# Forgetting attention of a two-block kernel: probabilities scaled before the product with the values, or the product scaled after it

## The reference, cut to what matters

```python
for i in range(S // Q_BLOCK):                      # four query tiles of 128
    logits = einsum("bqhd,bkhd->bhqk", qb, kb) * scale
    logits = logits + cum[:, :, q0:kl, None] - cum[:, :, None, :kl]
    p = jax.nn.softmax(jnp.where(mask, logits, NEG_INF), axis=-1)
    outs.append(einsum("bhqk,bkhd->bqhd", p.astype(vb.dtype), vb))
...
u = jax.nn.silu(layer_norm(causal_depthwise_conv(a * sigmoid(g)), ...))
return jnp.concatenate([u, att], axis=-1) @ w_out
```

## Time and profile before

| what | value |
|---|---|
| median of 3 runs | 1826.43 us (1825.73 to 1826.66) |
| the profiled execution | 1825.45 us |
| its span, first to last instruction | 1823.7 us |
| TensorE busy in the span | 1778.4 us (98%) |
| VectorE, ScalarE, GpSimd busy | 57%, 25%, 59% |
| mean granted TensorE clock | 0.992 |
| the attention loop on TensorE | 122.1 us to 211.9 us |
| TensorE busy in it | 79.32 of 89.80 us |

### The profile page before, as it was taken

The page is one execution under the profiler, slowest core; times in us unless marked ns, Lnnn a source line. Parts: engine busy times, 40 slices in busy tenths (PEclk is TensorE's granted clock), DMA queues, the critical chain, the costliest instruction groups (busy, mean ns, idle before and its releaser), DMA issues.

```text
span 1823.7 us, 22550 instructions
## 1 busy us (share of the span) xinstructions
PE 1778.4 (98%) x8332; PEld 1442.7 (79%) x8332; DVE 1030.7 (57%) x1194; ACT 463.7 (25%) x931; POOL 1074.9 (59%) x604
## 2 busy tenths in 40 slices
PE   9998999999999999999999999999999999999997
PEld 7775777788888877767888888887888888888886
DVE  5989465845252675175625261696766562616177
ACT  6427334401010122163201020212336320202011
POOL 7593453566666665434666666675344566666672
PEclk9999999999999999999999999999999999999999
DMA  6231221233333332212332333332122233332331
GB/s 239 70 103 48 81 78 39 81 102 94 93 102 93 94 102 92 82 47 59 92 104 92 96 100 92 98 99 81 52 66 69 79 95 93 100 97 92 103 93 47
DMA packets 46591, 161.44 MB, mean 89 GB/s; under 512 B 5232, under 2 KB 7792, under 8 KB 46384
## 3 DMA queue, kind: packets, MB, share of 16 engines
q1 hardware_dynamic: 45088, 157.31, 28.3%
q10 hardware_dynamic: 1424, 3.02, 0.5%
HBM read 158.21 MB, written 2.10 MB: 88 GB/s over the span
## 4 chain that ended last, share of the span: by engine, by line
PE 92%; DVE 4%; ACT 2%; issue 1%; DMA 0%; POOL 0%; SPq 0%; DVEq 0%; ACTq 0%
PE bank L405 21%; PE bank L407 21%; PE bank L406 21%; PE bank L453 3%; PE bank L455 3%; PE bank L454 3%; PE bank L1031 1%; PE bank L1001 1%; PE bank L473 1%; PE bank L474 1%; PE bank L475 1%; PE bank L1003 1%; PE bank L1002 1%; DVE bank L1768 1%; PE bank L1046 1%
## 5 line engine op out<-in xcount | busy, mean ns | idle before, releaser
L319 POOL TENSOR_TENSOR WL<-RAW,WH 128x1024 fp32r<-128x1024 f32 x291 | 740.1, 2543 | 24.3
L314 POOL TENSOR_SCALAR WH<-RAW 128x1024 fp32r<-128x1024 f32 x291 | 313.9, 1079 | 680.2 <-PE bank L407 362.7
L405 PE MATMUL bank<-AH,WH 128*128 128x512 f32 x848 | 332.6, 392 | 0.0
L406 PE MATMUL bank<-AL,WH 128*128 128x512 f32 x848 | 330.0, 389 | 0.0
L407 PE MATMUL bank<-AH,WL 128*128 128x512 f32 x848 | 330.0, 389 | 0.0
L405 PE MATMUL bank<-HH,WH 128*128 128x512 f32 x832 | 325.0, 391 | 0.0
L406 PE MATMUL bank<-HL,WH 128*128 128x512 f32 x832 | 323.8, 389 | 0.0
L407 PE MATMUL bank<-HH,WL 128*128 128x512 f32 x832 | 323.7, 389 | 0.0
L1421 ACT ACTIVATE TMP<-bank 128x512 f32<-128x512 f32 x96 | 57.3, 596 | 776.7 <-PE bank L407 738.9
L2043 DVE TENSOR_TENSOR HL<-TMP,HH 128x512 fp32r<-128x512 f32 x96 | 238.9, 2488 | 3.9 <-ACT HH L1426 0.7
L2049 DVE TENSOR_TENSOR Y<-Y,bank 128x512 f32<-128x512 f32 x72 | 49.5, 687 | 309.0 <-PE bank L407 309.0
(11 more groups left out here) (388 smaller groups left out, 2371.9 us busy)
## 6 DMA issues: line engine op xcount, KB each, us to landing
RAW<-wstream SPq DMA_DIRECT2D x291, 512.0 KB, 3.6
out<-Y SPq DMA_DIRECT2D x8, 256.0 KB, 2.3
X<-xT SPq DMA_DIRECT2D x3, 512.0 KB, 8.5
TMP<-memT ACTq DMA_DIRECT2D x1, 1024.0 KB, 7.5
MIX<-bands ACTq DMA_DIRECT2D x1, 768.0 KB, 4.6
RAW<-wstream SPq DMA_DIRECT2D x2, 256.0 KB, 3.8
X<-xT SPq DMA_DIRECT2D x2, 256.0 KB, 4.2
BF<-masks ACTq DMA_DIRECT2D x1, 352.0 KB, 3.7
```

Of the source, the lines that this page charges most:

```text
L314: nc.gpsimd.tensor_scalar(WH[:, s, :, :].rearrange("p k n -> p (k n)"), RAW[:, s, :], 1.0, 1.0, ALU.mult, ALU.mult).then_inc(sem("w_high"), 1)
L319: nc.gpsimd.tensor_tensor(WL[:, s, :, :].rearrange("p k n -> p (k n)"), RAW[:, s, :], f32(WH[:, s, :, :].rearrange("p k n -> p (k n)")), A ...
L405: mm(bank, WH[:, slot, k, :], h(k), start=(k == 0), stop=False)
L406: mm(bank, WH[:, slot, k, :], l(k), start=False, stop=False)
```

## The change

The exponentials are transposed and multiplied by the values as they are. VectorE takes the reciprocals of a whole pair's eight row sums in one instruction (iterations 4, 8, 12, 16). TensorE makes rows of them: eight small matmuls for a pair (`fox_factors`, iterations 5, 9, 13, 17), whose stationary operand is a column of SUMI repeated 64 times and whose moving operand is the identity, so that bank FOX_R holds in each head's 64 partitions the factor of every query. ScalarE copies that bank to TMP (`fox_fcopy`, iterations 6, 10, 14, 18), VectorE multiplies FOX_O by it into FOX_R (`fox_normed`, iterations 7, 11, 15, 19), ScalarE takes the high part from there (`fox_out`, same iterations) and VectorE the low part one iteration later (`fox_split`). The next pair's products now wait for `fox_normed`.

Since FOX_R is bank 6 for three pairs, the gate has bank 7 alone: ScalarE's last exponential of tile c waits until u of tile c-1 is split. The twelve matmul triples of the output projection come in another order, those into bank 6 last and behind a wait for the third pair. Four more convolution taps run ahead of the loop (FRONT_TAPS 32 in place of 28). In ScalarE's iterations the convolution's tail now comes ahead of the pair's output.

```diff
--- before.py
+++ after.py
@@ -63,7 +63,9 @@
 MLPS = ["m3", "f0", "f1"]
...
 FOX_S, FOX_T, FOX_O = (4, 5, 2), 0, 1
-FRONT_TAPS = 28
+FOX_R = (6, 6, 6, 2)
+OUT_PIECES = (((0, 0), (0, 1), (0, 2)), ((0, 3), (2, 0), (2, 1)), ((2, 2), (2, 3), (1, 0)), ((1, 1), (1, 2), (1, 3)))
+FRONT_TAPS = 32
 K_BANKS = (3, 4, 1, 2)
...
 OUT_FILL = 15
@@ -93,7 +95,6 @@
 SIDE_SECOND = 6
...
 POOL_QUADS = 7
-ACT_SCALED = 6
 FAMILIES = {
...
     "ah": each(["m1", "mm", "m2", "m3", "b", "f0", "c", "f1"], "ah", 8),
@@ -118,7 +119,7 @@
...
     "exp": [(f"{p}_exp", n) for p, n in ATTS],
-    "probs": [("fox_probs", 2 * (16 - ACT_SCALED)), ("mem_probs", 16), ("dif_probs", 16)],
+    "probs": [("mem_probs", 16), ("dif_probs", 16)],
     "trans": [("fox_trans", 32), ("mem_trans", 16), ("dif_trans", 16)],
...
     "pv": [("fox_pv", 16), ("mem_pv", 16), ("dif_pv", 16)],
@@ -212,7 +213,7 @@
         VC = sb("VC", [P, NVEC])
...
         MAXI = sb("MAXI", [P, 8])
-        SUMI = sb("SUMI", [P, 8])
+        SUMI = sb("SUMI", [P, 16])
         RC = sb("RC", [P, 4])
...
@@ -626,11 +627,12 @@
                 n = U0["out"]
...
                 pe.wait_ge(sem("u_low"), nth("u_low", 4))
-                for k in range(4):
-                    if k % 2 == 0:
-                        pe.wait_ge(sem(f"raw_split{k // 2}"), nth(f"raw_split{k // 2}", n // 4 + 1))
-                    pe.wait_ge(sem("u_low"), nth("u_low", k + 1))
-                    for j in range(3):
+                pe.wait_ge(sem("raw_split0"), nth("raw_split0", n // 4 + 1))
+                pe.wait_ge(sem("raw_split1"), nth("raw_split1", n // 4 + 1))
+                for piece in OUT_PIECES:
+                    for j, k in piece:
+                        if j == 1 and k == 0:
+                            pe.wait_ge(sem("fox_low"), nth("fox_low", 3))
                         wh = WH[:, k // 2, 4 * (k % 2) + j, :]
...
                         mm(B[OUT_BANKS[j]][:], wh, AH[:, k, :], start=(k == 0), stop=False)
@@ -652,13 +654,24 @@
                     pe.wait_ge(sem("m1_v_read"), nth("m1_v_read", 4))
...
                     pe.wait_ge(sem("fox_tcopy"), nth("fox_tcopy", 2 * j + half))
-                if j < ACT_SCALED:
-                    pe.wait_ge(sem("fox_scaled"), nth("fox_scaled", 2 * j + half + 1))
-                else:
-                    pe.wait_ge(sem("fox_probs"), nth("fox_probs", 2 * (j - ACT_SCALED) + half + 1))
+                pe.wait_ge(sem("fox_exp"), nth("fox_exp", 2 * j + half + 1))
                 for kb in range(fox[j][2] // P):
...
                 last.then_inc(sem("fox_trans"), 1)
+
+            def fox_factors(p):
+
+                pe.wait_ge(sem("fox_recip"), nth("fox_recip", p + 1))
+                if p == 0:
+                    pe.wait_ge(sem("conv"), nth("conv", 4 * CONV_W - 2 * SIDE_TAPS + 2))
+                elif p < 3:
+                    pe.wait_ge(sem("fox_low"), nth("fox_low", p))
+                for qt in range(TT):
+                    for half in range(2):
+                        n = 8 * (p % 2) + 2 * qt + half
+                        last = mm(B[FOX_R[p]][64 * half:64 * half + 64, qt * P:(qt + 1) * P],
+                                  SUMI[:, n:n + 1].to_broadcast([P, 64]), IDENT[:], start=True, stop=True)
+                last.then_inc(sem("fox_factor"), 1)
...
                 if i < len(fox):
@@ -693,7 +706,7 @@
                 if 0 <= j < len(fox):
...
                     if j % 4 == 0 and p:
-                        pe.wait_ge(sem("fox_low"), nth("fox_low", p))
+                        pe.wait_ge(sem("fox_u"), nth("fox_u", p))
                     pe.wait_ge(sem("fox_tcopy"), nth("fox_tcopy", 2 * j + 2))
...
                         for half in range(2):
@@ -703,6 +716,8 @@
                     last.then_inc(sem("fox_pv"), 1)
...
                     next(filler, None)
+                if i >= 5 and i % 4 == 1:
+                    fox_factors((i - 5) // 4)
...
             def quad_then_units(name, count, h, l, ready, read, banks=(0, 1, 2, 3, 4, 5, 0, 1)):
@@ -1329,19 +1344,25 @@
                 c = i - LN_GATE - 1
...
                     act.wait_ge(sem("su_arg"), nth("su_arg", c + 1))
-                    if c < 2:
+                    if c == 0:
                         act.wait_ge(sem("ln_norm"), nth("ln_norm", 4))
                     else:
-                        act.wait_ge(sem("u_low"), nth("u_low", c - 1))
-                    nc.scalar.activation(B[6 + c % 2][:], Y[:, c, :], ACT.Exp).then_inc(sem("su_done"), 1)
+                        act.wait_ge(sem("u_low"), nth("u_low", c))
+                    nc.scalar.activation(B[7][:], Y[:, c, :], ACT.Exp).then_inc(sem("su_done"), 1)
                 c = i - LN_GATE
...
+            def fox_fcopy(m):
+                act.wait_ge(sem("fox_factor"), nth("fox_factor", m + 1))
+                if m:
+                    act.wait_ge(sem("fox_u"), nth("fox_u", m))
+                nc.scalar.activation(TMP[:, 5, :], B[FOX_R[m]][:], ACT.Copy).then_inc(sem("fox_fcopy"), 1)
+
             def fox_out(m):
-                act.wait_ge(sem("fox_pv"), nth("fox_pv", 4 * (m + 1)))
-                nc.scalar.activation(HH[:, 4 + m, :], B[FOX_O][:], ACT.Copy).then_inc(sem("fox_high"), 1)
+                act.wait_ge(sem("fox_u"), nth("fox_u", m + 1))
+                nc.scalar.activation(HH[:, 4 + m, :], B[FOX_R[m]][:], ACT.Copy).then_inc(sem("fox_high"), 1)
...
@@ -1352,21 +1373,14 @@
                     act.wait_ge(sem("fox_pv"), nth("fox_pv", j - 1))
...
-            def fox_scale(j):
-                n, kl = 2 * j % 8, fox[j][2]
-                act.wait_ge(sem("fox_recip"), nth("fox_recip", j + 1))
-                for half in range(2):
-                    p0 = FP[half][:, j % 3, 0:kl]
-                    nc.scalar.activation(p0, p0, ACT.Copy, scale=SUMI[:, n + half:n + half + 1]).then_inc(sem("fox_scaled"), 1)
-
-            for i in range(len(fox) + 3):
+            for i in range(len(fox) + 4):
                 j = i - 2
...
                     fox_tcopy(j, 0)
-                if 1 <= i <= ACT_SCALED:
-                    fox_scale(i - 1)
                 if i < len(fox):
                     kl = fox[i][2]
+                    if i >= 8 and i % 4 == 0:
+                        act.wait_ge(sem("fox_factor"), nth("fox_factor", i // 4 - 1))
                     if i == 1:
...
                     if i >= 3:
@@ -1374,7 +1388,7 @@
                     for half in range(2):
...
                         act.wait_ge(sem("fox_max"), nth("fox_max", n + 1))
-                        nc.scalar.activation(FP[half][:, i % 3, 0:kl], B[FOX_S[n % 3]][:, 0:kl], ACT.Exp, bias=MAXI[:, n % 8:n % 8 + 1], accum_out=SUMI[:, n % 8:n % 8 + 1]).then_inc(sem("fox_exp"), 1)
+                        nc.scalar.activation(FP[half][:, i % 3, 0:kl], B[FOX_S[n % 3]][:, 0:kl], ACT.Exp, bias=MAXI[:, n % 8:n % 8 + 1], accum_out=SUMI[:, n % 16:n % 16 + 1]).then_inc(sem("fox_exp"), 1)
                 if 0 <= j < len(fox):
...
                 if i == MV_READ[0]:
@@ -1384,9 +1398,11 @@
                 if i == MV_READ[1]:
...
                     nc.scalar.activation(MV[:, 1, :], B[3][:], ACT.Copy, scale=ST[:, 1:2]).then_inc(sem("m1_mv_read"), 1)
+                conv_tail(i)
                 if i >= 6 and i % 4 == 2:
-                    fox_out((i - 6) // 4)
-                conv_tail(i)
+                    fox_fcopy((i - 6) // 4)
+                if i >= 7 and i % 4 == 3:
+                    fox_out((i - 7) // 4)
...
@@ -1906,18 +1922,23 @@
                 c = i - LN_GATE - 2
...
                     dve.wait_ge(sem("su_done"), nth("su_done", c + 1))
-                    u = B[6 + c % 2][:]
+                    u = B[7][:]
                     own(v.tensor_tensor(u, SG[:, c, :], u, ALU.mult).then_inc(sem("u_done"), 1), "u_done")
...
+            def fox_normed(m):
+                dve.wait_ge(sem("fox_pv"), nth("fox_pv", 4 * (m + 1)))
+                dve.wait_ge(sem("fox_fcopy"), nth("fox_fcopy", m + 1))
+                done(v.tensor_tensor(B[FOX_R[m]][:], B[FOX_O][:], TMP[:, 5, :], ALU.mult).then_inc(sem("fox_u"), 1), "fox_u")
+
             def fox_split(m):
                 dve.wait_ge(sem("fox_high"), nth("fox_high", m + 1))
-                done(v.tensor_tensor(HL[:, 4 + m, :], B[FOX_O][:], f32(HH[:, 4 + m, :]),
+                done(v.tensor_tensor(HL[:, 4 + m, :], B[FOX_R[m]][:], f32(HH[:, 4 + m, :]),
                                      ALU.subtract).then_inc(sem("fox_low"), 1), "fox_low")
...
             fox = fox_steps()
-            for i in range(len(fox) + 4):
+            for i in range(len(fox) + 5):
                 if i < len(fox):
...
                         n = 2 * i + half
@@ -1927,22 +1948,15 @@
                         done(v.tensor_reduce(MAXI[:, n % 8:n % 8 + 1], B[FOX_S[n % 3]][:, 0:fox[i][2]],
...
                 if i >= 7 and i % 4 == 3:
-                    fox_split((i - 7) // 4)
+                    fox_normed((i - 7) // 4)
+                if i >= 8 and i % 4 == 0:
```

(20 more changed lines are left out.)

## The result

| | before | after |
|---|---|---|
| median of 20 runs each | 1825.66 us (1822.65 to 1826.87) | 1828.02 us (1825.30 to 1832.78) |
| ratio of the runs | | 1.0017, 95% interval 1.0011 to 1.0023 |
| profiled execution's span | 1823.7 us | 1828.0 us |
| the loop on TensorE | 122.12 to 211.88, 89.76 us | 122.44 to 214.56, 92.12 us |
| TensorE idle in it | 10.48 us | 10.09 us |

The account below looks back on a forecast made before the run. TensorE, busy 1778.4 of 1823.7 us, was taken as the bound. Its lateness went +1.1 (factors), +1.5 (chain), +2.6 (factors), +1.35 (wait removed), +2.45 (factors); 1826.43 + 2.4 = 1828.8 us, range 1824.8 to 1832.0.

Parts of the forecast that it names:

- iteration 12, second transposes: TensorE idles 3 us there for ScalarE's transposed copy, in place of the removed 2.82; lateness +1.5 us.
- Factor groups: Eight fp32 matmuls per pair on TensorE in iterations 5, 9, 13, 17: 1.09 us each, 4.4 us for four.
- rival C: Factor matmuls' repeated column loads slowly, 1.6 us in place of 1.09: +1.5, 1830.3 us; chance 0.08 with other delays.
- Pair 0's factors hidden, iteration 8 where it was: Iteration 5's factor group (1.1 us) is paid with idle time, so iteration 8 starts when it did.
- a sign of a misreading: Iteration 8 starting over 0.5 us away from 161.47 would mean what holds iterations 5 to 8 was misread.
- Iteration 10, +1.1: Pair 1's factors make TensorE start iteration 10 later by 1.09 us, at 171.45.
- The chain in iterations 10 to 12: With the gate's one bank, ScalarE and VectorE run one after the other; TensorE idles 3 us in iteration 12.
- Iteration 11's argument: VectorE instruction at about 179.9, up to 0.4 us later beside GpSimd's high part; forecast to take 0.7 us.
- rival B: Iteration 11's argument meets GpSimd's subtraction and waits its whole 2.35 us: about +2.0, 1830.8 us; chance 0.17.
- The clock behind the wait: Iteration 12's new wait is as long as the one removed, so the clock's loss behind it stays.
- The 1.26 gone: TensorE's wait of 1.26 us in iteration 13, ahead of iteration 14's transposes, goes; lateness falls to +1.35.
- Behind the loop nothing: Reordered output pieces and the last pair's chain, about 2.3 us beside other matmuls, add nothing after the loop.

Follow-up runs that it names:

- after_again: The changed kernel (after) run again unchanged; median 1828.72 us, ratio 1.0012 to before.
- e2: From after: each pair's factor matmuls issued twice into the same place; 1831.42 us, ratio 1.0037 to before.
- e5: From after: 28 convolution taps ahead of the loop, as in before, in place of 32; 1827.61 us, ratio 1.0017 to before.
- e1: From after: ScalarE's last gate exponential written in place to SBUF, so it waits for no bank or split; 1824.28 us, ratio 0.9996 to before.
- e3: From before: the gate's exponentials use bank 7 alone, each waiting for the split of the tile before; 1827.03 us, ratio 1.0008 to before.
- e6: From after: ScalarE's factor copy and the pair's high part go ahead of the convolution's tail; 1827.11 us, ratio 1.0011 to before.
- e4: From before: ScalarE scales the probabilities in all 16 steps, VectorE in none; 1825.22 us, ratio 0.9999 to before.
- e7: From after: e1's gate exponential in place together with e6's order of the two copies; 1824.81 us, ratio 0.9998 to before.
- e9: From e8: VectorE takes a pair's reciprocals ahead of its iteration's gate work; 1824.68 us, ratio 1.0002 to before.
- e8: From after with e1's edit: the factor copy moved from ScalarE to VectorE, ahead of its iteration's maxima; 1825.15 us, ratio 0.9994 to before.

## Why the prediction was right

1828.8 us was forecast, 1828.02 measured; against the median of before in the same runs it is +2.36 where +2.4 was forecast. That close an agreement is luck: the ratio of the same runs says +3.1, and after_again +2.2 by its ratio and +3.6 by the medians. The step by step account is less exact, and two of its errors cancel. TensorE's lateness against before, in the two first profiles (after's loop itself begins 0.32 us later):

| point | forecast | measured |
|---|---|---|
| iteration 8 | 0 | -0.83 |
| iteration 10 | +1.1 | 0.0 |
| iteration 12, second transposes | +1.5 | +0.7 |
| iteration 14 | +2.6 | +3.2 |
| iteration 15 | +1.35 | +1.8 |
| the loop's end | +2.45 | +2.7 |

- **Factor groups:** 0.97 us for 1.09, and e2 gives 0.88 for one more. Right, and rival C (1.6) is out: a repeated column as the stationary operand costs no more than a stored one.
- **Pair 0's factors hidden, iteration 8 where it was:** the mechanism right, the point wrong by more than the 0.5 us that the prediction named as a sign of a misreading. Iteration 8 came 0.83 us early, most of it because before's profile has a stretch at the low clock from 139 to 143 us and after's has none. In after_again, which has it, iteration 8 starts 39.09 us into the loop, against before's 39.35. What is worked out from one execution carries that execution's clock. What holds TensorE there is, as forecast, VectorE's second sum, which starts when the key projection ends: it ended 37.12 us into the loop in before and 36.86 in after_again. Only its wait was read wrongly. In before the statistic of iteration 7 had next to none, it started 0.06 us behind the sum; in after it waits 0.65, because TensorE waits less in iterations 5 and 6 (0.25 and nothing, for 0.67 and 0.26). The sum and the statistic in before, then the sum in after:

```profile
156.50 2.74 DVE L1889 TENSOR_TENSOR TMP<-Y 128x512 f32<-128x512 f32 x1
...
159.30 1.12 PE L689 MATMUL bank<-TMP,ONES 128*128 128x512 f32 x2
```

```profile
155.66 2.75 DVE L1905 TENSOR_TENSOR TMP<-Y 128x512 f32<-128x512 f32 x1
```

- **Iteration 10, +1.1:** the same 0.83. From iteration 8 to 10 the two profiles differ by 0.84: one factor group (0.97), less 0.03 of a wait and 0.10 that isn't assigned.
- **The chain in iterations 10 to 12:** right. From iteration 10's start the split of the first tile was forecast to end at 4.95 and ended at 4.96, the factor copy 7.85 and 8.02, the next split 11.15 and 11.46, the high part 14.05 and 14.52; the wait 3.0 and 3.06. The gap of up to 0.47 builds up in part over the hand-overs from one engine to the other, which I had at nothing and which take 0.10 us each (the product at 178.49 starts 0.10 behind the factor copy's end, the next exponential 0.10 behind the split's).
- **Iteration 11's argument, and rival B:** 0.68 us, as forecast, but with luck. The argument started at 179.09 and GpSimd's subtraction at 179.13; the forecast had 0.1 to 0.5 us between them and could not have told 0.04 from its opposite. The order does repeat: in after_again, e2 and e5 the argument was first by 0.02, 0.03 and 0.04 us. It was GpSimd's instruction that was held:

```profile
179.13 2.89 POOL L320 TENSOR_TENSOR WL<-RAW,WH 128x1024 fp32r<-128x1024 f32 x1
```

- **The clock behind the wait, "left as it was":** mis-sized. In both profiles of after it was low for 6.8 us behind the 3.06, against 3.4 us behind before's 2.82. From the second transposes to iteration 14's start TensorE worked 5.96 us at the low level against 2.51; half of the difference, 1.7, is lost. That is the +3.2 at iteration 14: the stretch took 8.78 us against 6.29, 0.97 of the 2.5 by the factors. In e2 and e5, with the same wait, it was low for 3.4 us only. In the first profile the missing early stretch pays the 1.7 back.
- **The 1.26 gone:** right; lateness fell by 1.44 there.
- **Behind the loop nothing:** right. The instructions are the same, and no wait of TensorE there is new. The spans still differ by 4.3 us where the loop's ends differ by 2.7. That is the clock of the two single executions: from the loop's end to 1815 us it was low for 17.1 us in before's profile and 20.5 in after's. Half of the 3.4 more, 1.7 us, is about the 1.6 that is left.

In the sum, after's loop is 2.8 us longer than before's at full clock: 3.2 of TensorE's work more and 0.4 of idle time less. Four factor groups are 3.9 of that work. The other 0.7 was saved around removed waits, where rows that count as busy were stretched too: 0.5 around iteration 6's 0.26 and 0.2 around the 1.26 of iteration 13. The 4.1 us of waits for scalings came back almost whole (0.90 and 3.06) by another way, as forecast; e1 shows that this way, not the factors, decides between a loss and a tie.

**Which version is best?** None beats before: those with e1's edit lie at 0.9994 to 1.0002. They win idle time and clock, and hand it to the factors. At the same mean granted clock of the execution, 0.993, before's mean is 1824.1 us (16 executions) and e1's 1824.3 (6); after has 1826.6 (2), and at 0.992 1828.1 (10) to before's 1825.2 (50).

## What to carry to other kernels

When a change takes a wait off the bounding engine, look at what the two engines beside it must hand each other in that stretch: if the new order makes each wait for the other's last instruction, the chain's length is the sum of both queues, and here it could be added up from row durations to within half a microsecond before anything was run. A double buffer given up costs nothing where something else holds the bounding engine longer (e3), and decides the result once that is gone and more hand-overs have been hung on the same chain (after against e1 and e6). An experiment that adds a cost under a wait that covers it does not clear the cost. When an engine that feeds the bound has no gap left, moving or reordering its work moves the wait and does not shorten it (e4, e7, e9).

## What the runs showed of the hardware

- **Idle time and the clock.** In the loop's twelve profiles the granted clock is at its low level, 1.2 of 2.4 GHz, for 3.4 us or 6.8 us at a time. One follows the 2.3 us wait at the key projection, between 136 and 143.5 us, in ten of the twelve; after and e2 have that wait without it. One follows the wait of iteration 12 wherever this is 1.9 us or more (before 2.82, after 3.06 twice, e2 3.05, e3 2.45, e5 3.06, e6 1.92), and never where it is 1.3 or less (e1, e4, e7, e8, e9). Whether it lasts 3.4 or 6.8 us differs between kernels with the same wait (6.8 in after, 3.4 in e2 and e5).
- **One kernel's times spread with it.** The eleven executions of after_again go from 1825.57 us at a mean clock of 0.994 to 1831.17 at 0.990, in the order of their clock. A difference of 2 us between two single profiles is no finding.
- **Who starts first is decided by hundredths.** Of a VectorE instruction with two SBUF inputs and GpSimd's subtraction, the later one waits: VectorE first by 0.04 us (after), and it took 0.68 and GpSimd's 2.89; VectorE later by 0.18 us (e6), and it took 2.73 and GpSimd's 2.36.
